# A 256-token two-block model kernel: half of a transposed solution, half of a group norm and half of a row transpose each taken earlier or later

## What is computed

```python
def rwkv7_scan(r, decay, k, v, kk, a):
    def step(S, inp):
        r_t, w_t, k_t, v_t, kk_t, a_t = inp
        sa = jnp.einsum('bhij,bhj->bhi', S, -kk_t)
        S = (S * w_t[:, :, None, :]
             + sa[..., None] * (kk_t * a_t)[:, :, None, :]
             + v_t[..., None] * k_t[:, :, None, :])
        y = jnp.einsum('bhij,bhj->bhi', S, r_t)
        return S, y
...
    mean = jnp.mean(y, axis=-1, keepdims=True)
    var = jnp.mean(jnp.square(y - mean), axis=-1, keepdims=True)
    y = (y - mean) * lax.rsqrt(var + GN_EPS)
    y = y * lnx_w + lnx_b
    y = (y + bonus) * g
...
    x = x + concat(y, attention) @ l0_w_out
    x = x + sq_relu_mlp(rmsnorm(x, g_ffn), up, down)
```

## Time and profile before

| what | before |
|---|---|
| median of 3 runs | 962.73 us |
| the runs | 959.42, 962.73, 964.07 us |
| the profiled execution | 959.6 us, of which the span is 957.8 us |
| TensorE busy | 921.5 us, 96% of the span |
| VectorE busy | 642.8 us, 67% |
| ScalarE busy | 458.4 us, 48% |
| mean granted TensorE clock | 0.994 |

### The profile page before, as it was taken

The page is one execution under the profiler, slowest core; times in us unless marked ns, Lnnn a source line. Parts: engine busy times, 40 slices in busy tenths (PEclk is TensorE's granted clock), DMA queues, the critical chain, the costliest instruction groups (busy, mean ns, idle before and its releaser), DMA issues.

```text
span 957.8 us, 15427 instructions
## 1 busy us (share of the span) xinstructions
PE 921.5 (96%) x6358; PEld 792.3 (83%) x6358; DVE 642.8 (67%) x858; ACT 458.4 (48%) x658; POOL 73.5 (8%) x149
## 2 busy tenths in 40 slices
PE   6999999999999999999899999999999799999997
PEld 5888788899899988888688888888985588888886
DVE  5579788677768966746476656667655866666655
ACT  6445465434567444421364454545542755444453
POOL 6000000000110030000000000000553000000000
PEclk9999999999999999999999999999999899999999
DMA  9855444555665541000156665565893256566631
GB/s 324 250 183 176 132 165 144 176 176 188 219 199 176 179 130 45 1 1 3 45 176 219 193 204 176 176 192 160 251 229 90 68 174 220 176 190 207 196 111 44
DMA packets 106085, 152.42 MB, mean 159 GB/s; under 512 B 4114, under 2 KB 82464, under 8 KB 106016
## 3 DMA queue, kind: packets, MB, share of 16 engines
q1 hardware_dynamic: 101424, 141.19, 45.3%
q0 software_dynamic: 4272, 9.85, 3.8%
q10 hardware_dynamic: 320, 0.40, 0.1%
HBM read 145.58 MB, written 1.06 MB: 153 GB/s over the span
## 4 chain that ended last, share of the span: by engine, by line
PE 89%; DVE 6%; ACT 3%; issue 1%; DMA 0%; POOL 0%; SPq 0%; DVEq 0%; ACTq 0%; POOLq 0%
PE banks L1981 21%; PE banks L1934 14%; PE banks L1935 13%; PE banks L1936 13%; PE banks L1982 11%; PE banks L2324 4%; PE banks L2552 2%; DVE wl L1104 1%; PE banks L2412 1%; PE banks L2093 1%; PE banks L2117 1%; PE banks L2043 1%; ACT wh L656 1%; DVE x L1172 1%; PE banks L2423 1%
## 5 line engine op out<-in xcount | busy, mean ns | idle before, releaser
L1104 DVE TENSOR_TENSOR wl<-raw,wh 128x2048 fp32r<-128x2048 f32 x130 | 297.6, 2291 | 113.6 <-ACT wh L656 113.0
L656 ACT ACTIVATE wh<-raw 128x2048 fp32r<-128x2048 f32 x132 | 252.2, 1913 | 135.8 <-PE banks L1936 93.1
L1981 PE MATMUL banks<-x,wh 128*128 128x512 f32 x896 | 314.8, 394 | 0.0
L1982 PE MATMUL banks<-x,wl 128*128 128x256 f32 x896 | 250.5, 280 | 0.0
L1981 PEld LDWEIGHTS banks<-x,wh 128*128 128x128 f32 x896 | 168.2, 188 | 39.6 <-issue 3.0
L1982 PEld LDWEIGHTS banks<-x,wl 128*128 128x128 f32 x896 | 168.4, 188 | 1.1
L1934 PE MATMUL banks<-wh,yh 128*128 128x512 f32 x290 | 114.0, 393 | 3.0 <-DVE yl L1660 3.0
L1936 PE MATMUL banks<-wh,yl 128*128 128x512 f32 x290 | 112.5, 388 | 0.0
L1935 PE MATMUL banks<-wl,yh 128*128 128x512 f32 x290 | 112.5, 388 | 0.0
L1934 PE MATMUL banks<-x,wh 128*128 128x256 f32 x320 | 92.1, 288 | 1.8 <-DVE x L1172 1.7
L1936 PE MATMUL banks<-x,wl 128*128 128x256 f32 x320 | 90.1, 282 | 0.0
(11 more groups left out here) (375 smaller groups left out, 1248.5 us busy)
## 6 DMA issues: line engine op xcount, KB each, us to landing
raw<-in_l_ffn_up SPq DMA_DIRECT2D x32, 1024.0 KB, 5.5
raw<-in_l_ffn_down SPq DMA_DIRECT2D x32, 1024.0 KB, 4.9
raw<-in_w_in SPq DMA_DIRECT2D x29, 1024.0 KB, 5.1
raw<-in_l_w_in SPq DMA_DIRECT2D x13, 1024.0 KB, 5.1
raw<-in_l_pw SPq DMA_DIRECT2D x12, 1024.0 KB, 5.4
arena<-arena POOLq DMA_DIRECT2D x64, 71.0 KB, 4.2
raw<-in_w_out SPq DMA_DIRECT2D x4, 1024.0 KB, 5.1
raw<-in_l_w_out SPq DMA_DIRECT2D x4, 1024.0 KB, 5.0
```

The lines of the kernel that those rows point to most:

```text
L656: nc.scalar.activation(wh[:, u % WBUFS, :], raw[:, u % RAWS, :], ACT.Copy).then_inc(E("hi_split"), 1)
L1104: nc.vector.tensor_tensor(wl[:, u % WBUFS, :], raw[:, u % RAWS, :], wh[:, u % WBUFS, :].bitcast(F32), ALU.subtract).then_inc(E("lo_split"), 1)
L1981: mm(outs[t], h[:, k, c], x2[:, k, :, :].rearrange("p w t -> p (w t)"), start=k == 0, stop=False)
L1982: ins = mm(outs[t][:, 0:T], l[:, k, c], xh[:, k, :], start=False, stop=k == KC - 1)
```

## The change

Two things are done together.

The transposed solution: the transposes of half 0 (`states_transposed(0)`) now stand in the second pair's ZZ, ahead of its products, which write only half 1. Those of half 1 stand inside chunk 0, between received and the second state sum. WT becomes two tiles in other places (`ytmp` and the arena), with the banks 4 and 6; TensorE waits for half 1's copy only at chunk 4. S(0) moves to `thb` and is cleared before the inverse.

The group norm: ScalarE writes the high part of half 0 between the two roots, and VectorE its low part ahead of the second reciprocal. TensorE's `rwkv_part(0, 0)` is cut in two around the second spread. `rwkv_part(1, 1)` is cut in two around the first eight row transposes, and the second eight stand inside up0, after the first four pairs. VectorE now adds three quarters of the residual, then splits up0, makes the first two pairs of `xl`, adds the last quarter, and makes the rest.

```diff
-    s.use("wt0"), s.use("wt1")
+    s.use("wt0", 4), s.use("wt1", 6)
...
-        WT = chunks(slot(2))
+        WT = [ap.rearrange("p (c t) -> p c t", t=P) for ap in (ytmp[:, 0, :], arena[:, 2048:2560])]
...
+            if c == 0:
+                return thb[:, 1, 0:T]
...
+                    if (pair, name) == (1, "ZZ"):
+                        copy_out(WT[0], "wt0")
...
-            for i in range(2):
-                copy_out(WT[:, :, i * P:(i + 1) * P], f"wt{i}")
+            copy_out(WT[1], "wt1")
...
             group_deviation(0)
             group_squares(1)
-            group_deviation(1)
-            for t in range(NT):
+
+            def rwkv_high(t):
                 act.wait_ge(E("rwkv_out"), t + 1)
                 nc.scalar.activation(yh[:, 0:4, half(t)], centred[:, :, half(t)], ACT.Copy).then_inc(E("rwkv_hi"), 1)
+
+            rwkv_high(0)
+            group_deviation(1)
+            rwkv_high(1)
...
+            nc.vector.memset(S(0), 0.0).then_inc(E("state_zeroed"), 1)
             for pair in range(2):
                 for i, (name, who) in enumerate(INVERSE):
...
-            nc.vector.memset(S(0), 0.0).then_inc(E("state_zeroed"), 1)
-            dve.wait_ge(E("state_zeroed"), 1)
...
-                if c == 0:
-                    wait_empty(dve, "wt1")
...
             gate_and_shift(0)
+            rwkv_low(0)
             group_rstd(1)
-            rwkv_low(0)
...
-            add_residual("wp", units=((), (2,)), norm="f0")
...
+            add_quarter(0, 0), add_quarter(1, 0), add_quarter(0, 1)
+            next_unit()
+            split_norm("f0", (0, 1))
+            add_quarter(1, 1)
             split_norm("f0", (2, 3))
             next_unit()
...
                 for t, k in order:
+                    if between and (t, k) == (1, 0):
+                        between()
...
+                    if (pair, name) == (1, "ZZ"):
+                        wait_empty(pe, "ZZ_0"), wait_empty(pe, "ZZ_1")
+                        states_transposed(0)
...
-            for g in range(4):
-                wait_empty(pe, f"ZZ_{g}")
...
-            wait_empty(pe, "wt0"), wait_empty(pe, "wt1")
+            wait_empty(pe, "wt0")
...
+                if c == 4:
+                    wait_empty(pe, "wt1")
...
+                if c == 0:
+                    wait_empty(pe, "ZZ_2"), wait_empty(pe, "ZZ_3")
+                    states_transposed(1)
...
-            rwkv_part(0, 0)
+            rwkv_part(0, 0, range(2))
             unfold_group(1)
+            rwkv_part(0, 0, range(2, 4))
             rwkv_part(1, 0)
             rwkv_part(0, 1)
+            rwkv_part(1, 1, range(2))
             row_transposes("f0", "wp", 0)
-            rwkv_part(1, 1)
-            row_transposes("f0", "wp", 1)
+            rwkv_part(1, 1, range(2, 4))
...
+                        between = (lambda: row_transposes("f0", "wp", 1)) if (tag, i) == ("f0", 0) else None
+                        wide_unit(f"up{tag}_{i}", None if i else tag, between)
```

More of the change, by code:

```diff
@@ L1674, in _, with add_quarter @@
             rwkv_low(1)
-            add_residual("wp", units=((), (2,)), norm="f0")
+            def add_quarter(c, s):
+                name = f"wp{c}_{s}"
+                wait_full(dve, name)
+                nc.vector.tensor_tensor(xn[:, s, 512 * c:512 * c + 512], xn[:, s, 512 * c:512 * c + 512], bank(name), ALU.add)\
+                    .then_inc(empty(name), 1)
+            add_quarter(0, 0), add_quarter(1, 0), add_quarter(0, 1)
+            next_unit()
+            split_norm("f0", (0, 1))
+            add_quarter(1, 1)
             split_norm("f0", (2, 3))
@@ L1966, in t_unit, with wide_unit @@
                 give(ins, name)
-            def wide_unit(name, source=None):
+            def wide_unit(name, source=None, between=None):
                 u = unit[0]
@@ L2290, in _, with states_transposed @@
             pe.wait_ge(E("scaled_keys"), 3)
+            def states_transposed(tt):
+                out = take(f"wt{tt}")
+                for p in range(4):
+                    ins = nc.tensor.transpose(out[:, p * P:(p + 1) * P],
+                                              Z[:, 0, tt, 2 * p:2 * p + 2, :].rearrange("p h d -> p (h d)"), ident)
+                give(ins, f"wt{tt}")
             needs = {"AV": ("GA",), "N2": ("GD", "GN"), "D2": ("AV",), "N4": ("N2", "D2"), "X2": (), "D4": ("N4",),
@@ L2331, in _ @@
                         heads_step(HEAD_TURNS[turn], 16, 8)
-            for g in range(4):
-                wait_empty(pe, f"ZZ_{g}")
-            for tt in range(NT):
-                out = take(f"wt{tt}")
-                for p in range(4):
-                    ins = nc.tensor.transpose(out[:, p * P:(p + 1) * P], Z[:, 0, tt, 2 * p:2 * p + 2, :].rearrange("p h d -> p (h d)"), ident)
-                give(ins, f"wt{tt}")
-            wait_empty(pe, "wt0"), wait_empty(pe, "wt1")
+            wait_empty(pe, "wt0")
             pe.wait_ge(E("state_zeroed"), 1)
@@ L2356, in attention_part, with rwkv_part @@
                     ins.then_inc(E("unit_summed"), 1)
-            def rwkv_part(c, s):
+            def rwkv_part(c, s, ks=range(4)):
                 u = UID[("N", "l0_w_out_2", 0, 512 * c)]
-                if s == 0:
+                if s == 0 and ks[0] == 0:
                     arrived(u)
@@ L2365, in rwkv_part @@
                 rows = slice(s * P, (s + 1) * P)
-                for k in range(4):
+                for k in ks:
                     ins = three(bank(f"wp{c}_{s}"), yh[:, k, rows], yl[:, k, rows], h[:, k, :], l[:, k, :], False, k == 3)
-                give(ins, f"wp{c}_{s}")
+                if ks[-1] == 3:
+                    give(ins, f"wp{c}_{s}")
             def both_parities(one, n=4):
@@ L2417, in recalled @@
                     hp = HD * par
-                    return mm(outs[par][rows, p * HD:(p + 1) * HD], WT[hp:hp + HD, p, c * C:(c + 1) * C],
+                    return mm(outs[par][rows, p * HD:(p + 1) * HD], WT[tt][hp:hp + HD, p, pb:pb + C],
                               S(c)[hp:hp + HD, p * HD:(p + 1) * HD], start=True, stop=True)
@@ L2518, in ffn @@
                     if i < FF_STEPS:
-                        wide_unit(f"up{tag}_{i}", None if i else tag)
+                        between = (lambda: row_transposes("f0", "wp", 1)) if (tag, i) == ("f0", 0) else None
+                        wide_unit(f"up{tag}_{i}", None if i else tag, between)
                     if i == 0:
```

## The result

| | before | after |
|---|---|---|
| median, us (runs) | 962.65 (4) | 956.86 (4) |
| lowest to highest | 959.42 to 964.07 | 956.72 to 957.01 |
| profiled execution, us | 959.6 | 957.01 |
| its span, us | 957.8 | 955.2 |

The ratio is 0.9942, interval 0.9925 to 0.9960: the change takes 5.8 us off, faster by 0.58%. A second comparison, with other runs of both, gave 956.84 us and 0.9934 (0.9920 to 0.9948). The forecast was 958.0 us. Two executions of the kernel before near 981.5 us, out of the twelve of before_again (Experiment 1), are left out of its median and its ratio.

The account below looks back on a forecast made before the run. TensorE, busy 921.5 of 957.8 us, was taken as the bound, so only its waits could give time. 2.0 + 2.1 = 4.1 us took the profiled 959.6 to 955.5; median forecast 958.0 us, range 954.0 to 962.0.

Parts of the forecast that it names:

- Part A: Transposed solution, end of the inverse to chunk 0's second state sum: 2.0 us gained, bounds 1.0 and 2.04.
- The two meetings with under 0.1 us of room: Chunk 0: VectorE frees received's bank by 420.25, due 420.3; recalled's read-out lets TensorE go at 421.3 to 421.4, due 421.4.
- rival 3: Chunk 0: received waits for the last ZZ product's bank, moving the 0.98 us wait; total 3.3, 959.4 us; chance 0.04.
- Part B up to the output product: Group norm: `rwkv_part(0, 0)` starts 1.6 us earlier; the 0.85 us wait and the first residual-add wait go.
- Rival 4: Group norm: two more ScalarE table loads, 1.28 us each, for a copy between two roots; total 2.4, 960.3 us; chance 0.03.
- Part B into the MLP: up0 waits 1.1 us for banks, down0 0.9 us for ScalarE's chain; down0 2.1 us earlier, bounds 1.0 and 3.0.
- Rivals 1 and 2: First: TensorE alone leads, total 5.0, 957.0 us, chance 0.14. Second: MLP entrance gives less, total 2 to 3, 960.2 us, 0.15.
- the one from the sum to the median: Whole kernel: 4.1 us off median 962.73 gives 958.6, off the four-time average 961.5 gives 957.4; 958.0 taken between.
- rival 5: Output product or MLP start: waits left around up0 and up1 bring a clock fall; 18 us of it gives 967.6; chance 0.04.
- the paragraph on the monitor: Clock monitor runs free of the kernel, so the fall near 748 us may shift: up to 1.5 us either side.

Follow-up runs that it names:

- before_again: The kernel before, unchanged, run once more beside itself: median 962.84 us (959.50 to 965.66), ratio 0.9995.
- Experiment 1: Against the kernel before: transposed solution alone 958.74 us; group norm and MLP start alone 958.43; kernel before again 962.84; changed kernel again 956.84.
- Experiment 4: Changed kernel with ScalarE's four squares later 955.70 us; with row transposes in other banks than up0's 956.08; with both edits 955.16.
- Experiment 2: Two more profiles of the unchanged kernel before: one run's median 962.59 us (profiled execution 963.93), the other a single execution of 960.61 us.
- Experiment 3: Two useless products put in TensorE's 2.11 us wait: kernel before 960.79 us, ratio 0.9981; transposed solution alone 959.49 us, ratio 0.9968.
- c_both: Changed kernel with transposes f0_t0 to f0_t3 in banks 2 to 5 and ScalarE's four squares behind the second hidden value: 955.16 us, ratio 0.9933.

## Why the prediction was right, and where it was not

**What bounds the kernel.** Right: TensorE's waits moved, its busy time is 922.0 against 921.5 us.

**Part A**, 2.0 us with bounds 1.0 and 2.04: it gave 1.90. The two meetings with under 0.1 us of room were both met, received doesn't wait (rival 3 is out), the copy of half 0 and the clearing lie in cover. The tenth of a microsecond short is spread over distances between rows, no wait among them.

**Part B up to the output product.** Right in each step: the high part between the roots, the second spread without a wait, the third part and the residual adds without one. The low part was expected 1.6 us earlier, and the wait fell from 2.11 to 0.49. Rival 4 is out: one table load at 455.33 serves both roots.

**Part B into the MLP.** The waits were named with cause and place: 1.1 us for the banks ahead of up0 (measured 1.15), 0.9 with bounds of 0.5 and 1 ahead of down0 (measured 0.64). Experiment 4 shows both causes. B gave 2.20, expected 2.1. Rivals 1 and 2 (3.0 in B; 2 to 3 in all) are out.

**One number stated wrong.** The prediction said that from ZZ's last row to down0 it would be 72.1 instead of 76.2 us. It is 491.12 - 419.46 = 71.7. The four transposes that moved ahead of that row (0.45 us) are no longer behind it, so the row itself is a shifted mark, and the gain read from it would be half a microsecond too large. From a mark ahead of everything that moved, 77.96 became 73.85.

**The step that was off** is the one from the sum to the median. It took the profiled execution, 959.6 us, and shifted the result by 4.1 us from there and from the mean of four times, as if the executions of before differed by noise. They differ by falls of the clock, and the profiles of the change lack one of them: the one that follows the 2.11 us wait in two of the four profiles of before, 1.6 us (Experiment 2). That it is there in the usual execution of before is not shown by a trace; the filled wait (Experiment 3) speaks for it. Carried with that term, 962.7 - 4.1 - 1.6 gives 957.0, and 956.86 was measured. The text did weigh the clock, in rival 5 and in the paragraph on the monitor, but in one direction only: it asked whether the waits that stay could bring a fall, and took the 1.00 behind the 2.11 us wait in the earlier trace rows as evidence that such a wait is harmless. Of four traces two show that and two don't. It was the wrong row to generalise from, and the one hint against it stood in the table of times, in which that execution was among the fastest. Rival 1 had named 957.0 us, nearer to the result than the forecast, by a mechanism that the waits ahead of up0 and down0 rule out: that number is a coincidence. The forecast stayed 1.1 us from the result and inside its range, but the chance for faster by over 0.5% (0.40) was smaller than that for no change (0.56), and the result is 0.58%, with an interval (0.40 to 0.75%) on both sides of that line.

## What to carry to other kernels

Before the gain of a shortened wait is carried to the median, look whether the profiled execution is a typical one, and take two or three profiles of the kernel before: a wait can have a price in the clock beside its length (here 1.6 us behind 2.1 us of waiting, in two profiles of four), and one trace may show it without that price. Measure a moved stretch between two marks that did not move themselves. A long piece of work without a due time in an in-order queue (the unit split on VectorE) belongs behind the short instruction that TensorE is about to ask for; tried on c_both, that one move took 3.85 us off the median, more than half of what the whole change gave.

## What the hardware showed

A fall can outlast its cause by far. In the profile of before_again the clock fell right behind the two waits ahead of chunk 0 (1.1 and 0.8 us) and stayed at the 1.2 GHz level through the whole loop over chunks, with TensorE busy in every microsecond; windows:

```profile
418.00:422.00 4.00, 2.14 (x21) 1.77 (x21) 2.08 (x4) 1.09 (x2) 0.00 (x0) 0.97 0.00 0
422.00:447.00 25.00, 25.00 (x238) 19.48 (x237) 8.42 (x22) 0.00 (x0) 0.00 (x0) 0.50 0.01 1
447.00:473.00 26.00, 26.00 (x305) 21.79 (x302) 8.89 (x24) 2.51 (x2) 0.00 (x0) 0.50 0.01 2
473.00:477.00 4.00, 4.00 (x89) 3.20 (x89) 3.22 (x3) 0.63 (x1) 0.00 (x0) 1.00 0.00 0
```

51 us at half the clock, where all other falls in the profiles here last 3.4, 6.8 or about 10 us, apart from those that the kernel's end cuts off. The span is 979.9 us, 22 more than the 957.8 of the profile that the prediction was read from. before_again had two executions near 981.5 us among twelve, and no other run of any kernel here, before included, was above 966.1. Part A removes the two waits ahead of chunk 0; whether it keeps this from happening can't be told from something so rare. In these traces a fall also cost only what wasn't covered: the stretch of 3.4 us at 0.50 in the profile of before at 358.5 us cost nothing, because TensorE would have waited next, and the same length 7 us later in after cost 1.6 us.
